# A float32 encoder layer on one core: the opening of the first sequence is put in another order

## The reference

```python
h = rmsnorm(x, norm_mix)
z = h @ w_in                                   # 512 pooling channels, then q, k, v of 12 heads of 64
a = pool_mixer(z[..., :512]) @ w_up_pool       # differences of window means, mixed in four groups
b = attention_branch(z[..., 512:]) @ w_up_attn # rotation of q and k, then dilated sliding windows
gates = sigmoid(h @ w_gate + b_gate)
x = x + (g_a * a + g_b * b) @ w_out            # g_a and g_b are the halves of gates
h = rmsnorm(x, norm_ffn)
x = x + (silu(h @ w_ffn_gate) * (h @ w_ffn_up)) @ w_ffn_down
return rmsnorm(x, norm_final)
```

## Time and profile before

| | |
|---|---|
| median of 3 runs | 2546.5 us (2546.46 to 2548.43) |
| the profiled execution | 2546.46 us |
| its span (first to last instruction) | 2544.4 us |
| PE busy | 2500.2 us, 98% |
| POOL, DVE, ACT busy | 1707.2, 1285.7 and 1034.9 us |
| mean granted TensorE clock | 0.997 of full speed |

### The profile page before, as it was taken

The page is one execution under the profiler, slowest core; times in us unless marked ns, Lnnn a source line. Parts: engine busy times, 40 slices in busy tenths (PEclk is TensorE's granted clock), DMA queues, the critical chain, the costliest instruction groups (busy, mean ns, idle before and its releaser), DMA issues. The chain is left out here.

```text
span 2544.4 us, 33052 instructions
## 1 busy us (share of the span) xinstructions
PE 2500.2 (98%) x11936; PEld 2058.5 (81%) x11936; DVE 1285.7 (51%) x1784; ACT 1034.9 (41%) x2000; POOL 1707.2 (67%) x1269
## 2 busy tenths in 40 slices
PE   7999999999999999999999999999999999999998
PEld 6788878888888888888778888888888888888887
DVE  7753546654422222388877435556453222223758
ACT  5224554444433233345552345534454233233445
POOL 7666456544888888756577754564359888887543
PEclk9999999999999999999999999999999999999999
DMA  4544446472233333474453535565622333335534
GB/s 148 163 144 133 154 150 189 151 258 83 79 104 100 108 104 100 133 235 150 134 159 109 154 104 158 164 179 172 234 88 83 107 105 100 108 104 166 190 124 145
DMA packets 329024, 354.40 MB, mean 139 GB/s; under 512 B 30368, under 2 KB 236064, under 8 KB 327328
## 3 DMA queue, kind: packets, MB, share of 16 engines
q1 hardware_dynamic: 327136, 347.99, 43.1%
q10 hardware_dynamic: 1728, 4.30, 0.5%
HBM read 250.85 MB, written 101.38 MB: 138 GB/s over the span
## 5 line engine op out<-in xcount | busy, mean ns | idle before, releaser
L1209 PE MATMUL ps<-S,t_hi 128*128 128x512 f32 (+2 forms) x2340 | 919.0, 393 | 14.8 <-POOL t_lo L980 5.1
L1211 PE MATMUL ps<-S,t_lo 128*128 128x512 f32 (+2 forms) x2340 | 906.0, 387 | 0.0
L1210 PE MATMUL ps<-S,t_hi 128*128 128x512 f32 (+2 forms) x2340 | 905.2, 387 | 0.0
L1209 PEld LDWEIGHTS ps<-S,t_hi 128*128 128x128 f32 x2340 | 440.8, 188 | 111.1 <-issue 12.5
L1211 PEld LDWEIGHTS ps<-S,t_lo 128*128 128x128 f32 x2340 | 440.4, 188 | 89.7
L1210 PEld LDWEIGHTS ps<-S,t_hi 128*128 128x128 f32 x2340 | 441.2, 189 | 85.7 <-issue 1.0
L980 POOL TENSOR_TENSOR t_lo<-wraw,t_hi 128x512 fp32r<-128x512 f32 x185 | 247.9, 1340 | 211.5 <-ACT t_hi L1713 208.3
L980 POOL TENSOR_TENSOR t_lo<-wraw_ff,t_hi 128x512 fp32r<-128x512 f32 x225 | 292.5, 1301 | 82.2 <-ACT t_hi L1713 78.1
L980 POOL TENSOR_TENSOR t_lo<-R,t_hi 128x512 fp32r<-128x512 f32 x154 | 220.5, 1437 | 180.9 <-ACT t_hi L1713 180.8
L1713 ACT CAST t_hi<-wraw_ff 128x512 fp32r<-128x512 f32 x225 | 139.5, 623 | 369.3 <-PE ps L1211 368.0
L1209 PE MATMUL ps<-t_hi,d_hi 128*128 128x512 f32 x616 | 241.5, 392 | 1.1 <-POOL t_lo L980 0.9
(11 more groups left out here) (182 smaller groups left out, 3910.9 us busy)
## 6 DMA issues: line engine op xcount, KB each, us to landing
d_raw<-d_rows SPq DMA_DIRECT2D x154, 256.0 KB, 3.2
d_rows<-act_f SPq DMA_DIRECT2D x110, 256.0 KB, 2.1
wraw_ff<-w_ffn_up SPq DMA_DIRECT2D x44, 512.0 KB, 4.6
R<-w_ffn_down SPq DMA_DIRECT2D x88, 256.0 KB, 3.3
wraw<-w_in SPq DMA_DIRECT2D x42, 512.0 KB, 5.6
sp_rows<-gst SPq DMA_DIRECT2D x80, 256.0 KB, 2.4
wraw_ff<-w_ffn_gate SPq DMA_DIRECT2D x40, 512.0 KB, 5.0
wo_raw<-w_out SPq DMA_DIRECT2D x36, 512.0 KB, 3.5
```

The source lines that it names most:

```text
L1209: nc.tensor.matmul(o_ps, w[0], r[0], start=begins, stop=False, skip_group_check=True)
L1210: nc.tensor.matmul(o_ps, w[0], r[1], start=False, stop=False, skip_group_check=True)
L1211: return nc.tensor.matmul(o_ps, w[1], r[0], start=False, stop=ends, skip_group_check=True)
```

## The change

`FIRST_PARTS` now reads A11 0, A12 0, A11 1, A11 2, A12 1, A11 3, A12 2, A12 3 for its first eight, each in the bank that it had. ScalarE casts operand 0 behind two parts (not five), and then casts the other six parts in one piece, ahead of operand 2. VectorE makes the low parts 0 to 7 in one piece, ahead of the first high norm. GpSimd's queue is changed in two places: it makes S2 of pair 1 behind the low part of operand 9 (not ahead of it), and it makes S4 of pair 1 no longer. VectorE makes that one, behind low part 20. TensorE transposes part 10 behind product 9, not ahead of it. The first rotation is split: VectorE's reading half (cosines and shuffle) stays ahead of low part 27, and the other half goes behind it. The counts of the semaphores follow. Nothing else in the program differs.

```diff
--- before.py
+++ after.py
@@ -163,10 +163,10 @@
 OPENING = (0, 2, 7, 9, 1, 4, 3, 5, 6, 8, 10, 11, 12, 13)
 PLACE = {m: k for k, m in enumerate(OPENING)}
 IN_FRONT = 9
-FIRST_PARTS = ([(part, p) for p in range(4) for part in ("A11", "A12")]
+FIRST_PARTS = ([("A11", 0), ("A12", 0), ("A11", 1), ("A11", 2), ("A12", 1), ("A11", 3), ("A12", 2), ("A12", 3)]
                + [("S2", 0), ("A22", 0), ("S2", 1), ("S2", 3), ("S2", 2)] + [("S1", p) for p in range(4)]
                + [("S3", p) for p in (0, 1, 3, 2)] + [("A22", p) for p in (1, 2, 3)] + [("S4", p) for p in range(4)])
-FIRST_BANKS = (0, 1, 6, 2, 3, 4, 5, 7, 1, 2, 3, 4, 5, 7, 2, 3, 4, 7, 5, 4, 2, 7, 5, 4, 7, 5, 4, 7)
+FIRST_BANKS = (0, 1, 6, 3, 2, 5, 4, 7, 1, 2, 3, 4, 5, 7, 2, 3, 4, 7, 5, 4, 2, 7, 5, 4, 7, 5, 4, 7)
 PARTS_AT = (FIRST_PARTS, [(part, p) for p in range(4) for part in TR_ORDER])
 PART_AT = [{key: f for f, key in enumerate(parts)} for parts in PARTS_AT]
 TILES_AT = [{key: n for n, key in enumerate(keys)} for keys in ([(p, e) for e in range(2) for p in range(4)],
@@ -219,7 +219,7 @@
 
 
 PER_SEQ = {
-    "ssx_ready": 8, "stdx_ready": 8, "ss_ready": 16, "std_ready": 16, "xn_ready": 16, "mix_made": 11, "tr_full": 28, "shi_ready": 28, "s_ready": 28,
+    "ssx_ready": 8, "stdx_ready": 8, "ss_ready": 16, "std_ready": 16, "xn_ready": 16, "mix_made": 10, "tr_full": 28, "shi_ready": 28, "s_ready": 28,
     "fill_full": 16, "a21_ready": 5, "sum_made": 20, "hi2_ready": 31, "pure_ready": 21, "low_ready": 10,
     "t_made": PAIR_SUMS + 4 * KC, "thi_ready": N_OPS, "t_ready": N_OPS, "prod_done": N_OPS,
     "p1_copied": N_PAIRS, "sums_done": 5 * N_PAIRS,
@@ -1124,8 +1124,9 @@
                     second_pair_sum(s, 0)
                     mix_first(s, 0)
                     low_part(s, 7, next11)
-                    mix_first(s, 1)
+                    mix_s1(s, 1)
                     low_part(s, 9, next21)
+                    mix_s2(s, 1)
                     mix_first(s, 2)
                     low_part(s, 1, t2[:, :, :])
                     low_part(s, 4, t1[:, :, :])
@@ -1137,7 +1138,6 @@
                     fourth_pair_sum(s, 0)
                     mix_s4(s, 0)
                     low_part(s, 5, b21)
-                    mix_s4(s, 1)
                     low_part(s, 6, b22)
                 else:
                     first_pair_sum(s, 0)
@@ -1220,8 +1220,8 @@
                     m = mixed1[s][p]
                     src = {"A11": low[:, 0:H2], "A12": low[:, H2:D], "A22": high[:, H2:D]}
                     pe.wait_ge(xn_ready, due("xn_ready", s, TILES_AT[s][p, 0 if part in ("A11", "A12") else 1] + 1))
-                    if part in made and s == 0 and (p == 3 or (part, p) == ("S4", 2)):
-                        pe.wait_ge(last_made, made[part] if p == 3 else 5)
+                    if part in made and s == 0 and (p == 3 or part == "S4" and p):
+                        pe.wait_ge(last_made, made[part] if p == 3 else 7 - p)
                     elif part in made:
                         pe.wait_ge(mix_made, due("mix_made", s, mix_count(s, part, p)))
                     bank_read(b)
@@ -1458,9 +1458,9 @@
                     leading_rest(s, 0, 0)
                     pair_product(s, 2)
                     pair_product(s, 7)
-                    part_transposes(s, range(8, 11))
+                    part_transposes(s, range(8, 10))
                     pair_product(s, 9)
-                    part_transposes(s, range(11, 17))
+                    part_transposes(s, range(10, 17))
                     pair_product(s, 1)
                     part_transposes(s, range(17, 21))
                     pair_product(s, 4)
@@ -1917,12 +1917,11 @@
                 if s == 0:
                     for p in range(4):
                         first_stats(s, p, (0,))
-                    part_his(s, range(5))
+                    part_his(s, range(2))
                     operand_hi(s, 0)
-                    part_his(s, range(5, 7))
+                    part_his(s, range(2, 8))
                     operand_hi(s, 2)
                     first_stats(s, 0, (1,))
-                    part_his(s, range(7, 8))
                     first_stats(s, 1, (1,))
                     first_product(s, 0)
                     first_stats(s, 2, (1,))
@@ -2136,12 +2135,25 @@
                 dve.wait_ge(last_made, 2)
                 V_.tensor_tensor(s4, a12, s2, ALU.subtract).then_inc(last_made, 1)
 
-            def third_pair_fourth():
-
-                _, a12, _, _ = parts_of(xb[0][2])
-                _, s2, _, s4 = [a[:, :, :] for a in mixed1[0][2]]
-                dve.wait_ge(mix_made, mix_count(0, "S2", 2))
+            def fourth_sum_of(p):
+
+                _, a12, _, _ = parts_of(xb[0][p])
+                _, s2, _, s4 = [a[:, :, :] for a in mixed1[0][p]]
+                dve.wait_ge(mix_made, mix_count(0, "S2", p))
                 V_.tensor_tensor(s4, a12, s2, ALU.subtract).then_inc(last_made, 1)
+
+            def first_rope_read():
+
+                dve.wait_ge(prod_done, place(0, 2) + 1)
+                dve.wait_ge(tab_in, due("tab_in", 0, 2))
+                V_.tensor_tensor(first_c[:, :], ps[:, 0, :], rope_cos[:, half(0)], ALU.mult)
+                V_.stream_shuffle(first_sh[:, :], ps[:, 0, :], partner).then_inc(rope_read, 1)
+
+            def first_rope_made():
+
+                dve.wait_ge(rope_read, 1)
+                chain.link(V_.tensor_tensor(r_s[:, :], first_sh[:, :], rope_sin[:, half(0)], ALU.mult))
+                V_.tensor_tensor(qkst[0][0][:, half(0)], first_c[:, :], r_s[:, :], ALU.add).then_inc(qk_ready, 1)
 
             def second_norm(s, t):
 
@@ -2259,9 +2271,9 @@
                 if job:
                     dve.wait_ge(qk_ready, due("qk_ready", s, job))
                 else:
-                    dve.wait_ge(s_ready, due("s_ready", s, 28 if s else 27))
+                    dve.wait_ge(s_ready, due("s_ready", s, 28))
                     dve.wait_ge(tab_in, due("tab_in", s, 2))
-                r_c, r_sh = (ps[:, 4, :], ps[:, 5, :]) if s or job else (first_c[:, :], first_sh[:, :])
+                r_c, r_sh = ps[:, 4, :], ps[:, 5, :]
                 V_.tensor_tensor(r_c, ps[:, bank_of(s, n, c), :], rope_cos[:, half(h)], ALU.mult)
                 V_.stream_shuffle(r_sh, ps[:, bank_of(s, n, c), :], partner).then_inc(rope_read, 1)
                 dve.wait_ge(rope_read, due("rope_read", s, job + 1))
@@ -2505,9 +2517,8 @@
                 if s == 0:
                     for p in range(4):
                         first_norm(s, 2 * p)
-                    part_los(s, range(6))
+                    part_los(s, range(8))
                     first_norm(s, 1)
-                    part_los(s, range(6, 8))
                     for p in range(1, 4):
                         first_norm(s, 2 * p + 1)
                     last_pair_first()
@@ -2517,13 +2528,16 @@
                     last_pair_fourth()
                     part_los(s, range(14, 17))
                     after_product(s, 1)
-                    third_pair_fourth()
-                    part_los(s, range(17, 24))
+                    fourth_sum_of(2)
+                    part_los(s, range(17, 21))
+                    fourth_sum_of(1)
+                    part_los(s, range(21, 24))
                     after_product(s, 3)
                     after_product(s, 4)
                     part_los(s, range(24, 27))
-                    rope_job(s, 0, 0)
+                    first_rope_read()
                     part_los(s, range(27, 28))
+                    first_rope_made()
                 dve.wait_ge(const_in, 16 * 3)
 
                 for m in range(FRONT + 1):
```

## The result

The changed kernel takes 2553.73 us (median of 12 runs, 2550.95 to 2556.45) against 2547.9 for the kernel before on the same chip (12 runs, 2545.93 to 2552.96). The ratio on record, from all the runs, is 1.0019, with a 95% interval of 1.0012 to 1.0027: 4.8 us slower (3.1 to 6.9); the two medians by themselves lie 5.8 us apart. It is slower as forecast, but by more than twice the 2.0 us, and above the range, which ended at 2551.5. The profiled execution took 2553.28 us with a span of 2551.6, against 2546.46 and 2544.4 before.

What follows compares the result with a forecast made beforehand. TensorE, 98% busy, bounds the kernel; only its early idle time can move. Steps -1.6, +3.9, -0.1, +1.5, -1.3, -0.3, +0.2 and -0.3 total +2.0 us, from 2546.46 to 2548.5; range 2542.5 to 2551.5.

Steps and rivals of the forecast that it cites:

- Product 0 and product 2: Opening: the 1.80 us stall inside product 0 goes, and product 2 starts at 21.6 against 23.17, 1.6 us earlier.
- Product 7: Norms and GpSimd operations alternate ahead of low operand 7; product 7 starts at 29.8 against 27.47, 2.3 us late.
- The half clock within product 7: One low-clock stretch, about 1.5 us, within product 7 after TensorE's 5.4 us idle time; step to product 9 -0.1 us.
- rival 3: Clock falls again in products 9 and 1, and VectorE loses the turn at part 27: 2552.5 us; chance 0.07.
- Product 9 to product 1: Part 10 and its queue delay part 12; product 1 starts at 41.9 against 38.23, a step of +1.5 us.
- the turn between the third sum of pair 3 and low operand 4: Ahead of product 1: if they meet, part 12 is low at 42.4, not 41.2; the middle was taken.
- Products 1 to 5: No gap from product 1 to product 5: a step of -1.3 us, of which S4 is -1.1.
- The rotations: Ahead of product 12: second shuffle ends 5.05 us behind part 27's cast, VectorE first, or 6.05; product 12 2.0 late.
- the slack of 0.35 us: Spare time of VectorE's rotation chain ahead of product 12, subtracted from its lateness: a step of -0.3 us.
- the lost turn at part 27: Rotations: GpSimd's low operand 8 goes ahead of VectorE's second half; 1.0 us, counted in rival 3.
- rival 1: Norms do not hold up GpSimd, product 7 starts at 26.2: 3.5 us less, 2543.0 us; chance 0.17.
- rival 2: Losses and gains cancel, full speed in product 7, only the rotations' chain sets product 12: +0.3, 2546.8 us; chance 0.23.

Runs made afterwards that it cites:

- e1: The changed kernel with one more wait: VectorE's third high norm starts only after GpSimd's low operand 7; 2550.9 us, ratio 1.0006 to the kernel before.
- e10: The kernel before with only S4 of pair 1 moved from GpSimd to VectorE, behind part 20; 2547.65 us, ratio 0.9993 to the kernel before.
- e4: The kernel before with S4 of pair 1 by VectorE and the first rotation split, its second half behind pair 1's sum v; 2544.75 us, ratio 0.9986.
- e6: The changed kernel with the split rotation's second half moved behind the sum v of pair 1; 2548.39 us, ratio 1.0000 to the kernel before.
- e9: The kernel before with only the first rotation split, its second half right behind low part 27; 2550.43 us, ratio 1.0004 to the kernel before.
- e2: The kernel before with only the new opening: order of eight parts, operand 0 behind two casts, low parts ahead of norms; 2551.61 us, ratio 1.0009.
- e5: The changed kernel with part 10's transposes ahead of product 9 again; 2551.15 us, ratio 1.0009 to the kernel before.
- e7: The changed kernel with operand 0 cast behind five part casts again, not two; 2553.36 us, ratio 1.0014 to the kernel before.

## Why the prediction was right in kind and wrong in size

- **Product 0 and product 2**: right. Counted from the first transposes product 2 is 1.57 us earlier (12.26 against 13.83); 1.6 was forecast. ScalarE idled for 1.08 us for the landing (1.2 forecast), the squares started 1.8 later after the 0.5 by which the tokens were late (1.7 forecast).
- **Product 7**: right. It started 2.28 us later from the first transposes, and 2.3 was forecast, with four norms and four GpSimd operations in strict turns (e1 takes two of the norms away, and 1.8 us with them). The trace agrees with the exclusion that the Trainium skill's SBUF — State Buffer page states in "Who interferes with whom": eight operations in a row, four norms of 2.08 to 2.12 us and four of GpSimd of 2.12 to 2.26, where e1's took 1.27 with no norm beside them. VectorE got each of its four turns.
- **The half clock within product 7**: too small. I took one stretch as in the earlier trace rows, and 0.1 us less from 7 to 9. It lasted 6.8 us and covered all of product 7: +0.95 from 7 to 9 instead of -0.1. No row of before had an idle time that long, so how long the half clock would last behind it was not known, and the forecast took the short length alone. No rival had this either: rival 3 put products 9 and 1 at half clock, and both ran at full speed. Why a stretch lasts 3.4 or 6.8 us stays open. This term was 1.05 us short.
- **Product 9 to product 1**: the step was seen and undersized. +1.5 was forecast, +2.27 came. The path was right: product 1 starts when part 12 is low. I gave the turn between the third sum of pair 3 and low operand 4 half its price, and it was lost in full (1.78 us against 0.71 in e1), which is 0.5 us. Without that turn it would have been 6.7 us from product 9 to product 1, as in e1, where the forecast had 6.4. 0.8 us short.
- **Products 1 to 5**: right. -1.3 was forecast, -1.37 came (e10).
- **The rotations**: the step that failed. I took the shuffle 5.05 us behind the cast of part 27, VectorE being first; it ended 6.15 behind (60.39 to 66.54), the other end that I had worked out (6.05). My own rows had GpSimd first, by 1.18 against 1.3 us, and I chose against them; it was first by 0.04 us, and VectorE's two operations took 1.79 and 1.64. This is 1.1 us. No run has the other order in this place, so its price rests on these rows; what the half on the chain costs as a whole is shown by e4, e6 and e9. Two smaller terms came with it: I had part 27's cast 3.25 us behind product 5, where it is 3.50 in the earlier trace rows and 3.49 here, and of the slack of 0.35 us 0.2 were used. From 5 to 12 it is +1.08, where the forecast had -0.4. 1.5 us short.
- Together 2.0 + 1.05 + 0.8 + 1.5 = 5.35, less 0.1 for the terms that were right, is the 5.2 us of the table (66.50 - 61.29). The span grew by 7.2: 0.55 is the tokens' later landing, and 1.4 came behind product 12, where half-clock stretches last 6.8 us (from 653 and 1913) in one trace and 3.4 (from 647 and 1282) in the other. These differ from run to run in one kernel, and only the profiled executions show them, so how much of the 4.8 us they are stays open.
- **The range** reached 3 us above the forecast, less than the three undersized terms (3.3) together. All of them were on the same side. Two, the turns at the third sum and at the rotation, were bounds that I had written down and then halved or passed over; the longer half clock was not written down. The forecast also started from 2546.5, the median of three runs, where 12 runs of the kernel before have 2547.9, and those beside the experiments 2548.7 to 2549.5. These 1.4 us are part of the 5.2 by which the median lies above the forecast.
- The rivals: no gain came (rival 1), the losses did not cancel (rival 2), and of rival 3 the lost turn at part 27 came, but not the half clock in products 9 and 1.

## What to carry to other kernels

Where two engines exclude each other, what counts is which of their operations now lie side by side: with VectorE's norms in one block, two of them cost 1.8 us at product 7 (e1), and one more wait on VectorE brought it back. A stall taken off the queue that shows it is a gain only if the next chain has slack; here that chain (rotations that free the banks) had 0.35 us. Moving two operations off it took 2.4 us off the kernel before from product 5 to product 12 (e4), where splitting them in place added 1.2 (e9). For a transfer of work past a product, follow the queue of the engine that takes it over: what now stands ahead of the next product's operands, and beside what. The bank ahead of which the wait shows need not be what holds the product. And a bound that rests on which of two operations is issued first by 0.1 us belongs into the sum at its dear end, if the rows have the other engine first.

## What the runs showed of the hardware that was not expected

- Half-clock stretches came at lengths of 3.4 and of 6.8 us. A 5.2 us idle time was followed by 6.8 us in the changed kernel and in e2, e5 and e6 (4.73 us and again 6.8 in e7); one of 3.35 us by 3.4 (e1); the old opening, with idle times under 2 us, had 3.4 in two traces and 6.8 in three. What decides between the two is not shown.
- Product 7 wholly at half clock took 5.27 us (30.30 to 35.57) against about 2.75 at full speed.
